# RWKV-7 block inverse: levels 2 to 16 kept as 32x32 diagonal blocks and multiplied in four array positions

## The chip, the cores and the metric

One NeuronCore of a Trainium2 chip runs the kernel. The metric is the device time of one execution in microseconds (us), as the median of a few runs. Engines are named as in the profile: PE is TensorE's matmul stream, PEld its weight loads, DVE is VectorE, ACT is ScalarE, POOL is GpSimd and SP is SyncE, which issues the DMAs of the weight stream.

## What is computed

Two layers of a hybrid decoder trunk on 256 tokens, in float32. Each layer has one input projection that feeds three head groups (HGRN2, latent attention called MLA, RWKV-7), an output projection, and a SwiGLU FFN. Only the RWKV-7 recurrence matters for the change:

```python
def step(state, inp):
    r_t, w_t, k_t, v_t, kk_t, a_t = inp
    sa = jnp.einsum('bhvk,bhk->bhv', state, -kk_t)
    state = (state * w_t[:, :, None, :]
             + sa[..., :, None] * (kk_t * a_t)[..., None, :]
             + v_t[..., :, None] * k_t[..., None, :])
    return state, jnp.einsum('bhvk,bhk->bhv', state, r_t)
```

with 8 heads of 64 channels. The kernel cuts the 256 steps into 4 chunks of 64. Inside a chunk the dependence of `sa` on earlier `sa` is a system with a 64x64 unit lower triangular matrix, I + A, where A holds decayed products of `kk` with `kk*a`. The kernel needs (I + A)^-1 for 8 heads x 4 chunks = 32 such matrices in each layer.

## The kernel before

**Where the inverse lives.** A tile is 64 partitions (one of two heads) x 64 columns; 16 tiles lie side by side (`JC` = 16), and the two heads of a pair share the partitions 0 to 63 (`EVEN`) and 64 to 127 (`ODD`). All buffers named here are views of one SBUF tensor, so the trace calls them all `arena`: `mab` (A below the diagonal), `inv` (the inverse so far), `inv_t` (its transpose), `g_t` (an intermediate).

**How it is inverted.** First the 2x2 diagonal blocks are set up (L1452 to L1454). Then five levels, `RW_LEVELS = [2, 4, 8, 16, 32]`, each double the block size. A level k is two steps on PE: `level_g(k)` multiplies `mab` with `inv_t` into the PSUM banks 0 and 1, ACT copies this out with a factor of -1 (`gt_out(k)`, L800), `level_x(k)` multiplies `inv` with it into banks 2 and 3, and DVE writes the new blocks by a copy under a mask (`level(k)`, L1440) into `inv_t` and turns them into `inv` by 32x32 transposes (L1432). Each step goes in two halves of 8 tiles. For levels 2 to 16 (k = 0 to 3) the products are full 64x64 ones by `both_heads` (L1897), in two positions of the PE array: rows and columns 0 to 63 for the even head, 64 to 127 for the odd. Level 32 (k = 4) multiplies single 32x32 quarters by `quarters` (L1906), also in two positions. At levels 2 to 16 no nonzero value leaves the 32x32 diagonal blocks of a tile.

**What stands around it.** PE's order is written out by hand (L2009 to L2044): the level steps stand between the steps of latent attention (`k_turn`, `attend` L1852 and L1858, `p_turn` L1870, `mix` L1878 and L1879) and the RWKV products (`product` L1897, `stack` L1920). After `level_x(4)` follow the chunk loop (L2051) and then the output projection, whose matmuls stand at L1631 to L1633. DVE's order is at L1451 to L1491 (`score_add` L1335, `score_max` L1341, `probs` L1353 and L1358 between the levels), ACT's at L863 to L888 (`softmax` L762, `probs_out` L769, `mix_out` L775, `stacked` L786, and the sums `sa` at L885). Each engine runs its list in order and waits on semaphores; nothing overtakes. These three lines of ACT's list matter below:

```python
                mix_out(0)
                gt_out(3)
                probs_out(3)
```

`mix_out(0)` waits for `rw_ab_done`, which DVE gives after `probs(3)` (L1474). PE's `p_turn(1)` waits for DVE's `probs(1)`.

**Elsewhere** the kernel streams weights: SP loads `raw`, ACT rounds them to `w_hi` (L532), DVE takes the rest as `w_lo` (L1000), and PE multiplies three times. The ring of `w_hi` and `w_lo` has four halves and `raw` has four slots, so this work runs ahead by that much.

Of the kernel before, what the change touches and what calls it, by code (L numbers as in the profile page):

```python
# [29 lines left out]
U32 = mybir.dt.uint32  # L30
# [23 lines left out]
RC = 64  # L54
NC = SEQ // RC
JC = 4 * NC
# [61 lines left out]
def build(nc, stream, x_in, positions, params, consts, lora, gains, rows, out):  # L118
    with ExitStack() as ctx:
# [119 lines left out]
        g_t = at(RING_END + 9856, JC, RC)  # L239
        inv = at(RING_END + 10880, JC, RC)  # L240
# [16 lines left out]
        LOWER = [slice(32, 64), slice(96, 128)]  # L257

# [263 lines left out]
        def _(act):  # L522
# [75 lines left out]
            for l in range(DEPTH):  # L598
# [190 lines left out]
                def gt_out(k):  # L789
                    last = k == len(RW_LEVELS) - 1  # L790
                    for hf in range(2):
                        h8 = slice(8 * hf, 8 * hf + 8)
                        act.wait_ge(S("rw_gt_mm"), 10 * l + 2 * k + hf + 1)
                        if last:
                            g3 = bank(hf).rearrange("p (n t) -> p n t", n=8)
                            nc.scalar.activation(g_t[UPPER[0], h8, 32:64], g3[UPPER[0], :, 32:64], ACT.Copy, scale=-1.0)
                            nc.scalar.activation(g_t[UPPER[1], h8, 32:64], g3[UPPER[1], :, 32:64], ACT.Copy,
                                                 scale=-1.0).then_inc(S("rw_gt_ready"), 1)
# [82 lines left out]
                gt_out(4)  # L881
                stacked(2, k_st, 4)
# [86 lines left out]
        def _(dve):  # L969
# [87 lines left out]
            def tables():  # L1057
# [7 lines left out]
                v(cp(lev_lo, flipped))  # L1065
                v(cp(small[:, 202:204], small[:, 200:202].bitcast(I32)))
# [35 lines left out]
            for l in range(DEPTH):  # L1102
# [305 lines left out]
                v(tt(rw_a, rw_a, rw_kk, MUL))  # L1408
# [25 lines left out]
                def level(k):  # L1434
                    last = k == len(RW_LEVELS) - 1
                    for hf in range(2):
                        h8 = slice(8 * hf, 8 * hf + 8)
                        dve.wait_ge(S("rw_dinv_mm"), 10 * l + 2 * k + hf + 1)
                        if not last:
                            vs(nc.vector.copy_predicated(inv_t[:, h8, :], over(lev_up[:, k, :], 8, RC).bitcast(U32),  # L1440
                                                         bank(2 + hf).rearrange("p (n t) -> p n t", n=8)),
                               "rw_xt", 12 * l + 2 * k + hf + 3)
                            vs(turn_blocks(inv[:, h8, :], inv_t[:, h8, :]), "rw_x", 10 * l + 2 * k + hf + 3)
                        else:
                            d3 = bank(2 + hf).rearrange("p (n t) -> p n t", n=8)
                            for up in UPPER:
                                u(cp(inv_t[up, h8, 32:64], d3[up, :, 32:64]))
# [164 lines left out]
        def _(pe):  # L1612
# [81 lines left out]
            for l in range(DEPTH):  # L1694
# [205 lines left out]

                def quarters(b0, ns, left, right):

                    last = None
                    for m, n in enumerate(ns):
                        for h in range(2):
                            last = mm(bank(b0)[UPPER[h], m * RC + 32:(m + 1) * RC], left(h, n), right(h, n),  # L1906
                                      start=True, stop=True)
                    return last
# [4 lines left out]

                def tile_of(z):
                    return lambda hp, n: z[hp, n, :]
# [10 lines left out]
                def level_g(k):  # L1926
# [3 lines left out]
                    for hf in range(2):  # L1930
                        ns = range(8 * hf, 8 * hf + 8)
                        pe.wait_ge(S("rw_xt"), 12 * l + 2 * k + hf + 1)
                        if last:
                            quarters(hf, ns, lambda h, n: mab[LOWER[h], n, 0:32],
                                     lambda h, n: inv_t[LOWER[h], n, 32:64]).then_inc(S("rw_gt_mm"), 1)
                        else:
                            both_heads(hf, ns, tile_of(mab), tile_of(inv_t), RC).then_inc(S("rw_gt_mm"), 1)

                def level_x(k):
                    last = k == len(RW_LEVELS) - 1  # L1940
                    for hf in range(2):
# [5 lines left out]
                        if not last:  # L1947
                            both_heads(2 + hf, ns, tile_of(inv), tile_of(g_t), RC).then_inc(S("rw_dinv_mm"), 1)
                        else:
                            quarters(2 + hf, ns, lambda h, n: inv[UPPER[h], n, 0:32],  # L1950
                                     lambda h, n: g_t[UPPER[h], n, 32:64]).then_inc(S("rw_dinv_mm"), 1)
# [119 lines left out]
                for c in range(NC):  # L2071
# [5 lines left out]
                    if c == 0:  # L2077
                        pe.wait_ge(S("rw_xt"), 12 * ev)
# [173 lines left out]
```

## Time and profile before

| what | us |
|---|---|
| runs | 2317.67, 2314.88, 2312.14 |
| median | 2314.88 |
| profiled execution: its own time | 2312.1 |
| its span, first to last instruction | 2309.8 |
| outside the span | 2.3 |

The span is 2.3 us shorter than the execution's own time. The profile has a page (busy time of the engines, the chain of work that ended last, groups of instructions) and views on the trace: groups by line, a timeline in order of time, sums over stretches. A busy PE counts the way of the last result through the array as well (a 64x64 matmul's record lasts 219 ns although the next starts long before), so the cost of a group of matmuls is read from its start to the start of the next group, and waits are read from the starts too. A float32 matmul leaves two records for each matmul in the code; `x64` in a row of L1897 is 32 matmuls.

### The profile page before, as it was taken

To read this page: it belongs to the slowest core of one execution; us is meant where nothing else is said; L and a number is where in the kernel's file an instruction comes from. 1 tells how busy PE (TensorE), PEld (TensorE's weight loads), DVE (VectorE), ACT (ScalarE), POOL (GpSimd) and SP (SyncE) were. 2 spreads that over 40 slices of the span, in tenths; PEclk is the share of its full clock that TensorE was granted. 3 is DMA by queue.
4 is the path that set the end of the run, shared out by engine and by line. 5 is a ranking of instruction groups with operands and counts; after the bars stand their busy time and mean duration, and the time that the engine had idled before them with its cause. 6 is when DMAs were issued, how large, how long until landed. Compare 5 with 4: busy or idle time off the path is not lost.

```text
span 2309.8 us, 32601 instructions
## 1 busy us (share of the span) xinstructions
PE 2285.3 (99%) x13153; PEld 1890.2 (82%) x13153; DVE 1377.5 (60%) x1504; ACT 1112.5 (48%) x1378; POOL 35.7 (2%) x50
## 2 busy tenths in 40 slices
PE   8999999999999999999999999999999999999999
PEld 7888688888888888888888886888888888888887
DVE  5787677655555445555657857775555554455554
ACT  6554755544444344444445547465444443444443
POOL 0000100000000000000000001000000000000000
PEclk9999999999999999999999999999999999999999
DMA  8555306656655555666655543156566565556553
GB/s 322 187 187 179 131 21 209 219 210 218 221 215 214 188 199 207 219 226 222 236 201 184 190 166 109 39 202 217 204 218 227 206 218 188 194 212 227 216 210 137
DMA packets 89041, 450.05 MB, mean 195 GB/s; under 512 B 9888, under 2 KB 30976, under 8 KB 42720
## 3 DMA queue, kind: packets, MB, share of 16 engines
q1 hardware_dynamic: 88240, 444.67, 54.3%
q0 software_dynamic: 688, 3.78, 0.5%
q8 instruction: 83, 1.36, 0.2%
q14 instruction: 30, 0.25, 0.0%
HBM read 424.82 MB, written 23.59 MB: 194 GB/s over the span
## 4 chain that ended last, share of the span: by engine, by line
PE 95%; DVE 3%; ACT 1%; DMA 0%; issue 0%; SPq 0%; DVEq 0%; ACTq 0%
PE psum L1631 29%; PE psum L1633 29%; PE psum L1632 29%; PE psum L1802 2%; PE psum L1897 2%; PE psum L2051 1%; PE psum L1726 1%; PE psum L1852 1%; DMA x<-x_in_dram 0%; PE psum L1858 0%; PE psum L1665 0%; DVE arena L1408 0%; PE psum L1906 0%; DVE arena L1410 0%; DVE arena L1414 0%
## 5 line engine op out<-in xcount | busy, mean ns | idle before, releaser
L1000 DVE TENSOR_TENSOR w_lo<-raw,w_hi 128x1024 fp32r<-128x1024 f32 (+2 forms) x752 | 901.1, 1205 | 756.1 <-ACT w_hi L532 745.9
L532 ACT ACTIVATE w_hi<-raw 128x1024 fp32r<-128x1024 f32 (+2 forms) x752 | 783.6, 1045 | 1045.0 <-PE psum L1633 1042.9
L1631 PE MATMUL psum<-w_hi,hT_hi 128*128 128x512 f32 (+2 forms) x2128 | 820.2, 385 | 5.0 <-DVE w_lo L1000 5.0
L1633 PE MATMUL psum<-w_hi,hT_lo 128*128 128x512 f32 (+2 forms) x2128 | 816.8, 384 | 0.0
L1632 PE MATMUL psum<-w_lo,hT_hi 128*128 128x512 f32 (+2 forms) x2128 | 816.8, 384 | 0.0
L1631 PEld LDWEIGHTS psum<-w_hi,hT_hi 128*128 128x128 f32 x2128 | 400.5, 188 | 84.0 <-DVE w_lo L1000 4.2
L1633 PEld LDWEIGHTS psum<-w_hi,hT_lo 128*128 128x128 f32 x2128 | 400.4, 188 | 78.1
L1632 PEld LDWEIGHTS psum<-w_lo,hT_hi 128*128 128x128 f32 x2128 | 400.5, 188 | 77.3
L1631 PE MATMUL psum<-w_hi,act_hi 128*128 128x512 f32 x872 | 339.2, 389 | 0.0
L1632 PE MATMUL psum<-w_lo,act_hi 128*128 128x512 f32 x872 | 339.2, 389 | 0.0
L1633 PE MATMUL psum<-w_hi,act_lo 128*128 128x512 f32 x872 | 339.2, 389 | 0.0
L1632 PEld LDWEIGHTS psum<-w_lo,act_hi 128*128 128x128 f32 x872 | 163.7, 188 | 34.0
L1631 PEld LDWEIGHTS psum<-w_hi,act_hi 128*128 128x128 f32 x872 | 163.7, 188 | 33.9
L1633 PEld LDWEIGHTS psum<-w_hi,act_lo 128*128 128x128 f32 x872 | 163.7, 188 | 33.9
L1802 PE MATMUL psum<-raw,arena 128*128 128x384 f32 (+1 forms) x192 | 71.9, 525 | 0.4
L1802 PEld LDWEIGHTS psum<-raw,arena 128*128 128x128 f32 x192 | 35.3, 190 | 30.9 <-issue 11.8
L1897 PEld LDWEIGHTS psum<-arena 64*64 64x64 f32 x1536 | 46.7, 135 | 10.4 <-DVE arena L1417 4.0
L1897 PE MATMUL psum<-arena 64*64 64x64 f32 x1536 | 49.9, 219 | 4.7 <-DVE arena L1417 2.3
L1564 DVE TENSOR_TENSOR act_lo<-gain,act_hi 128x1024 f32 (+1 forms) x22 | 27.0, 1226 | 21.0 <-ACT act_hi L949 21.0
L1547 DVE SCALAR_TENSOR_TENSOR act_row<-psum,small,silu 128x512 f32<-128x512 f32 x44 | 30.9, 744 | 0.0
L1054 DVE TENSOR_TENSOR x<-x,psum 128x1024 f32<-128x1024 f32 x23 | 27.9, 1214 | 4.9 <-PE psum L1633 4.9
L1554 DVE STREAM_TRANSPOSE gain<-act_row 128x1024 f32<-128x1024 f32 x22 | 27.4, 1245 | 3.3 <-DVE act_row L1547 1.7
(316 smaller groups left out, 1107.8 us busy)
## 6 DMA issues: line engine op xcount, KB each, us to landing
raw<-stream_dram SPq DMA_DIRECT2D x360, 1024.0 KB, 4.8
bounce<-gain SPq DMA_DIRECT2D x164, 128.0 KB, 2.7
gain<-bounce SPq DMA_DIRECT2D x41, 512.0 KB, 3.3
raw<-stream_dram SPq DMA_DIRECT2D x16, 512.0 KB, 5.0
raw<-stream_dram SPq DMA_DIRECT2D x8, 768.0 KB, 6.3
raw<-stream_dram SPq DMA_DIRECT2D x8, 640.0 KB, 3.9
x<-x_in_dram SPq DMA_DIRECT2D x4, 512.0 KB, 9.3
lor<-lora_dram POOLq DMA_DIRECT2D x2, 832.0 KB, 10.8
```

What stands on the lines that cost most here:

```text
L532: nc.scalar.activation(w_hi[:, q % HALF_RING, 0:2 * w], raw[:, j % 4, hf * 2 * w:(hf + 1) * 2 * w], ACT.Copy).then_inc(hi_done, 1)
L1000: tt(w_lo[:, q % HALF_RING, 0:2 * w], raw[:, j % 4, hf * 2 * w:(hf + 1) * 2 * w], w_hi[:, q % HALF_RING, 0:2 * w].bitcast(F32), SUB).then_ ...
L1054: vs(tt(xs, xs, psum[:, b0:b0 + 2, :], ADD), "x_added", n_added)
L1547: last = stt(act_row.rearrange("p a b -> p (a b)").rearrange("p (n t r) -> p t n r", n=16, t=TT)[:, t], psum[:, 2 + t, :].rearrange("p (n ...
L1554: nc.vector.transpose(blocks.rearrange("p (q k n) -> p k q n", q=4, k=4), act_row.rearrange("p a b -> p (a b)").rearrange("p (k q n) -> p ...
L1564: tt(lo, moved.rearrange("p (b n e) -> p n b e", n=8, e=32), hi.bitcast(F32), SUB).then_inc(S("act_lo_ready"), 1)
L1631: mm(o, a_hi, w_hi[:, r, cols], start=(k == 0), stop=False)
L1632: mm(o, a_hi, w_lo[:, r, cols], start=False, stop=False)
L1633: last = mm(o, a_lo, w_hi[:, r, cols], start=False, stop=(k == n_k - 1))
L1726: last = mm(bank(b0)[half, n * RC:(n + 1) * RC], left[:, h, tok], right[:, h, tok], start=True, stop=True)
L1802: last = mm(psum[:, UP_BANK[c] + t, 0:w], src[:, k, t * P:(t + 1) * P], raw[:, c % 4, k * w:(k + 1) * w], start=(k == 0), stop=(k == nk - 1))
L1897: last = mm(bank(b0, 2)[hp, m * w:(m + 1) * w], left(hp, n), right(hp, n), start=True, stop=True)
```

## The change

The level steps 2 to 16 keep and multiply only the two 32x32 diagonal blocks of each tile. `inv`, its transpose (now a buffer of its own, `inv_d`) and `g_t` are 32 columns wide instead of 64: the 128 partitions are four quarters, and each holds one diagonal block.

- PE: `half_blocks` makes four 32x32 matmuls for each tile of 8, one in each of four array positions (partitions 32q to 32q+31 in, the same out), where `both_heads` made two of 64x64. Level 32 stays in `quarters`, with its operands at new places.
- ACT: `gt_out` copies 128x256 instead of 128x512. A new `inverse_out`, between `gt_out(4)` and `stacked(2)`, puts the diagonal blocks into `inv_t`: one copy of 128x512 with a factor for each partition, and two of 32x512. `inv_t` is complete after it, so `rw_xt` counts 13 instead of 12 in a layer.
- DVE: the set-up of the 2x2 blocks is an addition of 128x512 that makes the identity, two masked copies of 128x512 and one transpose of 128x512; it was a product and a scalar_tensor_tensor of 128x1024 and a transpose of 128x1024. In the levels the masked copy and the transpose are 128x256 instead of 128x512. The factor -1 moves out of `gt_out` and of `rhs` into `rw_a`: `tensor_tensor` becomes `scalar_tensor_tensor` there, and `rhs` is a plain copy. Once at the start of the program the two halves of the level masks are added (128x128).

```diff
-        g_t = at(RING_END + 9856, JC, RC)
-        inv = at(RING_END + 10880, JC, RC)
+        HB = RC // 2
+        g_t = at(RING_END + 9856, JC, HB)
+        inv = at(RING_END + 10880, JC, HB)
+        inv_d = at(RING_END + 10880 + JC * HB, JC, HB)
...
+        QUARTER = [slice(32 * q, 32 * q + 32) for q in range(4)]
+        IN_HALF = [slice(32 * (q % 2), 32 * (q % 2) + 32) for q in range(4)]
...
                         if last:
-                            g3 = bank(hf).rearrange("p (n t) -> p n t", n=8)
-                            nc.scalar.activation(g_t[UPPER[0], h8, 32:64], g3[UPPER[0], :, 32:64], ACT.Copy, scale=-1.0)
...
                         else:
-                            nc.scalar.activation(g_t[:, h8, :].rearrange("p a b -> p (a b)"), bank(hf),
-                                                 ACT.Copy, scale=-1.0).then_inc(S("rw_gt_ready"), 1)
+                            nc.scalar.activation(g_t[:, h8, :], g3, ACT.Copy).then_inc(S("rw_gt_ready"), 1)
+
+                def inverse_out():
+
+                    act.wait_ge(S("rw_xt"), 13 * l + 10)
+                    nc.scalar.activation(inv_t[:, :, 0:32], inv_d, ACT.Copy, scale=C("strict_up")[:, 32:33])
+                    for low in LOWER:
+                        last = nc.scalar.activation(inv_t[low, :, 32:64], inv_d[low], ACT.Copy)
+                    last.then_inc(S("rw_xt"), 1)
...
                 gt_out(4)
+                inverse_out()
                 stacked(2, k_st, 4)
...
+                v(tt(lev_up[:, :, 0:32], lev_up[:, :, 0:32], lev_up[:, :, 32:64], ADD))
...
-                v(tt(rw_a, rw_a, rw_kk, MUL))
+                v(stt(rw_a, rw_a, -1.0, rw_kk, MUL, MUL))
...
                         if not last:
-                            vs(nc.vector.copy_predicated(inv_t[:, h8, :], over(lev_up[:, k, :], 8, RC).bitcast(U32),
-                                                         bank(2 + hf).rearrange("p (n t) -> p n t", n=8)),
-                               "rw_xt", 12 * l + 2 * k + hf + 3)
-                            vs(turn_blocks(inv[:, h8, :], inv_t[:, h8, :]), "rw_x", 10 * l + 2 * k + hf + 3)
+                            vs(nc.vector.copy_predicated(inv_d[:, h8, :], over(lev_up[:, k, 0:32], 8, HB).bitcast(U32), d3),
+                               "rw_xt", 13 * l + 2 * k + hf + 3)
+                            vs(turn_blocks(inv[:, h8, :], inv_d[:, h8, :]), "rw_x", 10 * l + 2 * k + hf + 3)
...
+                v(tt(inv, over(idst[:, 0:32], JC, HB), over(idst[:, 32:64], JC, HB), ADD))
                 dve.wait_ge(S("rw_m_mm"), 4 * l + 1)
-                v(tt(inv, bank(2, 2).rearrange("p (n t) -> p n t", n=JC), over(C("pair_lo"), JC, RC), MUL))
-                vs(stt(inv, inv, -1.0, over(idst, JC, RC), MUL, ADD), "rw_x", 10 * l + 1)
-                vs(turn_blocks(inv_t, inv), "rw_xt", 12 * l + 1)
+                a3 = bank(2, 2).rearrange("p (n t) -> p n t", n=JC)
+                v(nc.vector.copy_predicated(inv, over(C("pair_lo")[:, 0:32], JC, HB).bitcast(U32), a3[:, :, 0:32]))
+                vs(nc.vector.copy_predicated(inv, over(C("pair_lo")[:, 32:64], JC, HB).bitcast(U32), a3[:, :, 32:64]),
+                   "rw_x", 10 * l + 1)
+                vs(turn_blocks(inv_d, inv), "rw_xt", 13 * l + 1)
...
-                dve.wait_ge(S("rw_xt"), 12 * ev)
+                dve.wait_ge(S("rw_xt"), 13 * ev)
...
-                    vs(ts(rhs.rearrange("p a b -> p (a b)"), bank(0)[:, 0:256], -1.0, None, MUL), "rw_rhs_ready", NC * l + c + 1)
+                    vs(cp(rhs.rearrange("p a b -> p (a b)"), bank(0)[:, 0:256]), "rw_rhs_ready", NC * l + c + 1)
...
+                def half_blocks(b, ns, left, right):
+
+                    last = None
+                    for m, n in enumerate(ns):
+                        for q, rows in enumerate(QUARTER):
+                            last = mm(bank(b)[rows, m * HB:(m + 1) * HB], left(q, n), right(q, n), start=True, stop=True)
+                    return last
...
-                            both_heads(hf, ns, tile_of(mab), tile_of(inv_t), RC).then_inc(S("rw_gt_mm"), 1)
+                            half_blocks(hf, ns, lambda q, n: mab[QUARTER[q], n, IN_HALF[q]],
+                                        lambda q, n: inv_d[QUARTER[q], n, :]).then_inc(S("rw_gt_mm"), 1)
...
-                            both_heads(2 + hf, ns, tile_of(inv), tile_of(g_t), RC).then_inc(S("rw_dinv_mm"), 1)
+                            half_blocks(2 + hf, ns, lambda q, n: inv[QUARTER[q], n, :],
+                                        lambda q, n: g_t[QUARTER[q], n, :]).then_inc(S("rw_dinv_mm"), 1)
```

The order of the engines' lists stays. On PE, at level 2 of the first layer (`level_g(0)`, `k_turn(1)`, `level_x(0)`), there stood before (line 1897 is `both_heads`, 1822 is `k_turn`):

```order
L1897 MATMUL psum<-arena 64x64 [waits rw_xt,rw_m_ready,rw_stacked]
L1897 MATMUL psum<-arena 64x64 x15
L1897 MATMUL psum<-arena 64x64 [waits rw_xt]
L1897 MATMUL psum<-arena 64x64 x15
L1822 MATMUL psum<-con,arena 128x128 [waits mla_rT_ready,mla_k_normed]
L1822 MATMUL psum<-con,arena 128x128 x7
L1897 MATMUL psum<-arena 64x64 [waits rw_m_ready,rw_x,rw_gt_ready]
L1897 MATMUL psum<-arena 64x64 x15
```

and now stand (line 1920 is `half_blocks`, 1836 is `k_turn`):

```order
L1920 MATMUL psum<-arena 32x32 [waits rw_xt,rw_m_ready,rw_stacked]
L1920 MATMUL psum<-arena 32x32 x31
L1920 MATMUL psum<-arena 32x32 [waits rw_xt]
L1920 MATMUL psum<-arena 32x32 x31
L1836 MATMUL psum<-con,arena 128x128 [waits mla_rT_ready,mla_k_normed]
L1836 MATMUL psum<-con,arena 128x128 x7
L1920 MATMUL psum<-arena 32x32 [waits rw_m_ready,rw_x,rw_gt_ready]
L1920 MATMUL psum<-arena 32x32 x31
```

Twice as many matmuls stand in each half, 32 for 16, with the same waits at the same places.

On ACT, at level 32 of the first layer, from the rounding of two weight halves (line 532) through `gt_out(4)` (796 and 797) and `stacked(2)` (786) to the first `sa` (885), there stood before:

```order
L532 ACTIVATE w_hi<-raw 128x1024 [waits half_used,raw_in0] x2
L796 ACTIVATE arena<-psum 32x8x32 [waits rw_gt_mm]
L797 ACTIVATE arena<-psum 32x8x32
L796 ACTIVATE arena<-psum 32x8x32 [waits rw_gt_mm]
L797 ACTIVATE arena<-psum 32x8x32
L786 ACTIVATE arena<-psum 64x8x64 [waits rw_stack_mm]
L786 ACTIVATE arena<-psum 64x8x64 x3
L885 ACTIVATE arena<-psum 128x256 [waits rw_sa_mm]
```

and now stand (808 and 810 are `inverse_out`, 790 is `stacked(2)`, 896 the first `sa`):

```order
L536 ACTIVATE w_hi<-raw 128x1024 [waits half_used,raw_in0] x2
L800 ACTIVATE arena<-psum 32x256 [waits rw_gt_mm]
L801 ACTIVATE arena<-psum 32x256
L800 ACTIVATE arena<-psum 32x256 [waits rw_gt_mm]
L801 ACTIVATE arena<-psum 32x256
L808 ACTIVATE arena<-arena,con 128x16x32 [waits rw_xt]
L810 ACTIVATE arena<-arena 32x16x32 x2
L790 ACTIVATE arena<-psum 64x8x64 [waits rw_stack_mm]
L790 ACTIVATE arena<-psum 64x8x64 x3
L896 ACTIVATE arena<-psum 128x256 [waits rw_sa_mm]
```

Three copies stand ahead of `stacked(2)`; the wait of the first of them is for the end of level 16.

## Rows read from the trace of the kernel before

**Rows 1.** The page: busy time of PE, and the chain that ended last, by engine.

```profile
PE 2285.3 (99%) x13153; PEld 1890.2 (82%) x13153; DVE 1377.5 (60%) x1504; ACT 1112.5 (48%) x1378; POOL 35.7 (2%) x50
...
PE 95%; DVE 3%; ACT 1%; DMA 0%; issue 0%; SPq 0%; DVEq 0%; ACTq 0%
```

**Rows 2.** Sums over the stretch in either layer: length, busy, then PE clock, DMA.

```profile
281.34:349.22 67.88, 64.72 (x1539) 58.45 (x1539) 51.27 (x91) 36.38 (x75) 0.00 (x0) 1.00 0.10 34
1429.69:1497.57 67.88, 64.72 (x1539) 58.45 (x1539) 51.28 (x91) 36.38 (x75) 0.00 (x0) 1.00 0.09 32
```

**Rows 3.** Timeline of PE, first layer: start us, length us, engine, line.

```profile
289.72 2.08 PE L1897 MATMUL psum<-arena 64*64 64x64 f32 x64 [0.25 <-ACT arena L786]
291.74 1.09 PE L1822 MATMUL psum<-con,arena 128*128 128x128 f32 x8
...
297.13 1.58 PE L1852 MATMUL psum<-arena 128*128 128x128 f32 x8
...
305.88 1.53 PE L1870 MATMUL psum<-con,arena 128*128 128x128 f32 x12
...
308.71 3.02 PE L1897 MATMUL psum<-arena 64*64 64x64 f32 x96 [0.22 <-DVE arena L1440]
311.66 0.87 PE L1870 MATMUL psum<-con,arena 128*128 128x128 f32 x6
...
314.62 0.38 PE L1879 MATMUL psum<-arena 128*128 128x128 f32 x2
314.84 0.60 PE L1878 MATMUL psum<-arena 128*128 128x256 f32 x2
...
319.85 2.08 PE L1897 MATMUL psum<-arena 64*64 64x64 f32 x64 [0.72 <-ACT arena L800]
...
326.69 1.20 PE L1906 MATMUL psum<-arena 32*32 32x32 f32 x64
327.82 2.08 PE L1897 MATMUL psum<-arena 64*64 64x64 f32 x64
...
338.04 0.63 PE L2051 MATMUL psum<-gain,arena 64*64 64x64 f32 x16
338.51 0.63 PE L2051 MATMUL psum<-arena,con 64*64 64x64 f32 x16
```

**Rows 4.** Groups by line and form, 281 to 350 us: busy us, mean ns.

```profile
L1440 DVE COPY_PREDICATED arena<-con,psum 128x512 f32<-128x512 uint32 x8 | 5.9, 735 | 1.3 <-PE psum L1897 0.9
L1432 DVE STREAM_TRANSPOSE arena<-arena 128x512 f32<-128x512 f32 x8 | 5.7, 712 | 0.3
L800 ACT ACTIVATE arena<-psum 128x512 f32<-128x512 f32 x8 | 4.5, 593 | 2.8 <-PE psum L1897 2.8
L1484 DVE TENSOR_SCALAR arena<-psum 128x256 f32<-128x256 f32 x4 | 1.7, 425 | 3.2 <-PE psum L2051 2.9 <-DVEq L1449 0.2
L885 ACT ACTIVATE arena<-psum 128x256 f32<-128x256 f32 x4 | 1.5, 384 | 11.5 <-PE psum L2051 11.5
L1453 DVE SCALAR_TENSOR_TENSOR arena<-arena,con 128x1024 f32<-128x1024 f32 x1 | 1.2, 1226 | 0.0
```

**Rows 5.** Timeline of DVE, from score_add(1) to level 4's first masked copy.

```profile
297.33 0.96 DVE L1335 TENSOR_TENSOR arena<-psum,con 128x768 f32<-128x768 f32 x1 [0.37 <-PE psum L1858]
...
303.99 0.96 DVE L1335 TENSOR_TENSOR arena<-psum,con 128x768 f32<-128x768 f32 x1 [0.56 <-PE psum L1858]
...
306.40 0.74 DVE L1440 COPY_PREDICATED arena<-con,psum 128x512 f32<-128x512 uint32 x1
```

**Rows 6.** Timeline of ACT: stacked(1); mix_out(0) and gt_out(3); stacked(2).

```profile
287.06 2.40 ACT L786 ACTIVATE arena<-psum 64x512 f32<-64x512 f32 x4
...
318.29 1.02 ACT L775 ACTIVATE hT_hi<-psum 128x1024 fp32r<-128x1024 f32 x1 [2.79 <-DVE arena L1474]
319.21 1.08 ACT L800 ACTIVATE arena<-psum 128x512 f32<-128x512 f32 x2
...
330.96 2.40 ACT L786 ACTIVATE arena<-psum 64x512 f32<-64x512 f32 x4 [1.77 <-PE psum L1920]
```

More of the change, by code:

```diff
@@ L793, in gt_out @@
                         act.wait_ge(S("rw_gt_mm"), 10 * l + 2 * k + hf + 1)
+                        g3 = bank(hf)[:, 0:8 * HB].rearrange("p (n t) -> p n t", n=8)
                         if last:
-                            g3 = bank(hf).rearrange("p (n t) -> p n t", n=8)
-                            nc.scalar.activation(g_t[UPPER[0], h8, 32:64], g3[UPPER[0], :, 32:64], ACT.Copy, scale=-1.0)
-                            nc.scalar.activation(g_t[UPPER[1], h8, 32:64], g3[UPPER[1], :, 32:64], ACT.Copy,
-                                                 scale=-1.0).then_inc(S("rw_gt_ready"), 1)
-                        else:
-                            nc.scalar.activation(g_t[:, h8, :].rearrange("p a b -> p (a b)"), bank(hf),
-                                                 ACT.Copy, scale=-1.0).then_inc(S("rw_gt_ready"), 1)
+                            nc.scalar.activation(g_t[UPPER[0], h8, :], g3[UPPER[0]], ACT.Copy)
+                            nc.scalar.activation(g_t[UPPER[1], h8, :], g3[UPPER[1]], ACT.Copy).then_inc(S("rw_gt_ready"), 1)
+                        else:
+                            nc.scalar.activation(g_t[:, h8, :], g3, ACT.Copy).then_inc(S("rw_gt_ready"), 1)
[5 more added lines that the diff above has]
+                    last.then_inc(S("rw_xt"), 1)
                 up_out(0)
@@ L1905, in quarters @@
                         for h in range(2):
-                            last = mm(bank(b0)[UPPER[h], m * RC + 32:(m + 1) * RC], left(h, n), right(h, n),
+                            last = mm(bank(b0)[UPPER[h], m * HB:(m + 1) * HB], left(h, n), right(h, n),
                                       start=True, stop=True)
@@ L1931, in level_g @@
                         ns = range(8 * hf, 8 * hf + 8)
[L1932 removed]
+                        pe.wait_ge(S("rw_xt"), 13 * l + 2 * k + hf + 1)
                         if last:
                             quarters(hf, ns, lambda h, n: mab[LOWER[h], n, 0:32],
[L1935 removed]
+                                     lambda h, n: inv_d[LOWER[h], n, :]).then_inc(S("rw_gt_mm"), 1)
                         else:
[L1937 removed]
+                            half_blocks(hf, ns, lambda q, n: mab[QUARTER[q], n, IN_HALF[q]],
+                                        lambda q, n: inv_d[QUARTER[q], n, :]).then_inc(S("rw_gt_mm"), 1)
                 def level_x(k):
@@ L1947, in level_x @@
                         if not last:
-                            both_heads(2 + hf, ns, tile_of(inv), tile_of(g_t), RC).then_inc(S("rw_dinv_mm"), 1)
-                        else:
-                            quarters(2 + hf, ns, lambda h, n: inv[UPPER[h], n, 0:32],
-                                     lambda h, n: g_t[UPPER[h], n, 32:64]).then_inc(S("rw_dinv_mm"), 1)
+                            half_blocks(2 + hf, ns, lambda q, n: inv[QUARTER[q], n, :],
+                                        lambda q, n: g_t[QUARTER[q], n, :]).then_inc(S("rw_dinv_mm"), 1)
+                        else:
+                            quarters(2 + hf, ns, lambda h, n: inv[UPPER[h], n, :],
+                                     lambda h, n: g_t[UPPER[h], n, :]).then_inc(S("rw_dinv_mm"), 1)
                 up(0)
@@ L2077, in _ @@
                     if c == 0:
-                        pe.wait_ge(S("rw_xt"), 12 * ev)
+                        pe.wait_ge(S("rw_xt"), 13 * ev)
                     elif c < NC - 1:
```

6 lines of the change are left out of this document (2 added, 4 removed).

## The prediction

> **What bounds the kernel now.** I read the page first. PE is busy 99% of the span and makes 95% of the chain that ended last [rows 1]. So a microsecond that PE's list loses is won, and one that another engine loses is won only where PE waits for it. The work that the change touches stands in one stretch of 67.88 us in either layer, with the same counts and sums to 0.01 us; what I find for the first layer counts twice. The granted clock is 1.00 there, the upper of TensorE's two levels, and the DMA engines are nearly idle [rows 2]. Next I read PE's timeline in the stretch. It is almost a list without gaps: it waits 0.25 us for ACT's `stacked(1)`, 0.22 at level 8 for DVE and 0.72 at level 16 for ACT's `gt_out(3)` [rows 3], and at a few other places. PE is thus the bound, but DVE is busy 51 of 68 us [rows 2] and stands close behind.
>
> **A step of a level on PE, before.** `level_g(0)` starts at 289.72 and the next group at 291.74: 2.02 us for 32 matmuls, 64 records [rows 3]. There are eight such steps in a layer (levels 2 to 16, g and x), 16 in all. The records come in rounds, one in each of the two array positions. In the chunk loop, where the shape doesn't change from group to group, 16 records take 0.47 us (338.04 to 338.51), so a round of 64 columns is 58.5 ns; 32 rounds are 1.87, and 0.15 is left for the change of shape at the start [rows 3].
>
> **The same step after.** 64 matmuls, 128 records of 32x32. The only rows with this shape are `quarters`: 64 records in two positions take 1.13 us (326.69 to 327.82), less 0.13 for the change of shape 1.00 us, or 31.3 ns for a round of two [rows 3]. A round of 64 columns costs 58.5 and one of 32 columns 31.3, so a column costs 0.85 ns and a round 4 ns besides: the time goes with the columns that stream through, and hardly with the number of instructions. The question is what a round of four positions costs, and no row shows one. Three values:
> - All four run side by side as two do now: 32 rounds of 31.3 ns are 1.00 us, the step 1.13.
> - All four run side by side but each position adds its own fixed part. With one position, 128 columns take 110 ns a record (two records, 314.62 to 314.84 [rows 3]), which is 109 by the 0.85 and thus 1 over; two positions are 4 over, so four may be some 10: 37 ns a round, the step 1.31.
> - Only two run at a time: 64 rounds, 2.00 us, the step 2.13.
> Rounds of two start within one column time of the other and keep their own pace; I see nothing in the rows that ties one position to the other but this small fixed part. I take 1.21, between the first two, as it lies nearest to the row with the same shape. PE's list then loses 8 x (2.02 - 1.21) = 6.5 us in each layer.
>
> Here a rule of the skill speaks against the change. The rows show two 32x32 positions with different rows of the array that write the same PSUM bank at 31.3 ns a round [rows 3], too short for one after the other, at 27 ns of columns each. The Trainium skill, TensorEngine Tiling (Array Packing), section Gotcha 1: PSUM Pressure, says that different row tiles cannot access the same PSUM bank simultaneously. By that rule the four would queue; by the rows they don't, and I hold with the rows.
>
> **What of the 6.5 us arrives.** I went through the stretch with the waits that each list has, and find five places.
> - Start. DVE's set-up before `mab` was two operations and a transpose of 128x1024 at about 1.23 us each, 3.7 in all; now four of 128x512 at 0.71 to 0.74, 2.9 [rows 4]. It gives `mab` 0.8 us sooner, but PE also waits for ACT's `stacked(1)`, which ends at 287.06 + 2.40 = 289.46 [rows 6], and starts at 289.72 now [rows 3]: 0.2 won.
> - After `level_x(0)`, `attend(1)` waits for `k_out(1)` on ACT, a copy of 128x1024 as `mix_out` is, 1.02 us [rows 6], that starts when `k_turn(1)` ends. `level_x(0)` covers it now with 2.0 us and will with 1.2: 0.1 to 0.2 lost.
> - `p_turn(1)`. From `score_add(1)` at 297.33 to the first masked copy at 306.40, DVE works through two `score_max`, two `probs` and three `score_add` with one wait of 0.56 [rows 5]: 8.5 us of work that the change does not shorten, and it starts when `attend(1)` is done. PE needs from `attend(2)` at 297.13 to `p_turn(1)`, half through the 1.53 us from 305.88 [rows 3], 9.5 us now and 9.5 - 1.6 = 7.9 after. So PE waits some 0.9 us: two steps give 0.7 instead of 1.6. The DVE chain takes the place of PE there.
> - Level 16. `gt_out(3)` stands behind `mix_out(0)` on ACT, and that waits for DVE's L1474, which follows `probs(3)`, `softmax(3)`, `probs_out(2)` and PE's `p_turn(2)`. From `p_turn(2)` at 311.66 to `level_x(3)` at 319.85 are 8.19 us [rows 3] of which PE's own work is not the bound; they stay, less 0.2 for the shorter `gt_out(3)`. Of the 0.8 us of `level_g(3)` 0.2 arrives: 0.6 lost.
> - Level 8. The wait of 0.22 before its second half shrinks with the shorter masked copy and gives 0.1 to 0.3, and the next three waits, on `gt_out(2)` and `probs(2)`, take 0.2 to 0.3 back: nothing.
> Sum: 6.5 + 0.2 - 0.15 - 0.9 - 0.6 = 5.05; I take 4.9 for small waits that I can't place.
>
> **The other edits.** The masked copies and transposes of the levels are half as long in elements. 128x512 takes 0.735 and 0.712; another operation of DVE takes 0.425 at 128x256 [rows 4], so I put them at 0.43 to 0.49. That saves DVE 0.5 us a level, of which only the wait at level 8 was on PE's path. `gt_out` falls from 0.59 to the 0.38 of `sa`, which has the same shape [rows 4]; PE waited for it only where counted. `inverse_out` is three copies on ACT, 0.59 for 128x512 and not less than 0.38 nor more than 0.6 for each of the two on 32 partitions: 1.4 to 1.8 us, ahead of `stacked(2)`. ACT sat idle for 1.77 us before `stacked(2)` until PE's `stack` was done [rows 6], so it is hidden to within 0.1. It opens with `rw_xt` at the end of level 16, long past. Behind it are queued `stacked(2)` and the first `sa`; DVE waits for it before `rhs`, which comes 2 us after. Without this cover each microsecond of it would stand before the chunk loop. The factor in `rw_a` costs nothing: scalar_tensor_tensor over 128x1024 takes 1.226 us [rows 4], as a tensor_tensor of that size would by DVE's 0.71 to 0.74 for half the elements. The plain copy for `rhs` is at worst the same. The mask addition runs once, under 0.4 us, while PE works on the first weights. After the stretch nothing changes but the start: the weight halves are rounded ahead of it by up to four, and PE's list stays the bound, so the gain is kept to the end.
>
> **The sum** against the profiled execution: 2312.1 - 2 x 4.9 = 2302.3 us. That execution lies 2.8 us below the median of the runs shown; the median I expect is 2314.9 - 9.8 = 2305.1.
>
> **Rivals.**
> 1. Four positions run side by side, but instructions come too slowly to feed them. The rows show 128 loads and matmuls in 1.00 us [rows 3] and no higher rate; at four positions it would be twice that. A pace of 45 to 50 ns a round of four gives a step of 1.57 to 1.73, and 3.6 to 2.6 us a layer: 2308 to 2310. For it: the rate is unseen. Against: time went with columns, so the present rate is no limit.
> The Trainium skill, TensorE: Matmul & The Clock Gate, section Wait — 56ns, not 53.3ns?, gives a floor of about 25 ns from matmul to matmul. Taken for a float32 matmul with its two records, that would be 1.6 us a step, an estimate that lies within this rival; taken for each record, the rows at 15.7 ns already deny it.
> 2. Only two positions run at a time. The step is 2.13 us, 0.9 us more on PE in a layer, against 0.2 won at the start, 0.2 at level 8 and 0.2 at level 16, with small waits gone: within 0.5 us, 2314 to 2316. For it: two is all the rows show. Against: nothing in them hints at a limit of two.
> 3. The positions queue up behind each other in the bank that they share, as the Gotcha says. 128 records of 27 + 2 ns are 3.8 us a step, 1.9 more; 16 steps cost 30, less some 3 for what other waits absorb: 2342. It turns from gain to loss at a step of 2.14 us, 15.7 ns a record, which is today's pace of two at a time; anything slower loses. For it: four writers to a bank are new. Against: two writers show no queue.
> 4. The change does what it says on PE but DVE and ACT give nothing: the `probs(1)` chain decides more than I think. It runs from `attend(1)` alone, so it can take at most the 1.6 us of two steps, another 0.7 us a layer: 2306.5, inside the forecast's range.
>
> **Chances.** The forecast with four side by side (steps of 1.13 to 1.31 us and rival 4) 0.68: 2302 to 2308 with the runs' own spread. Rival 1 0.12, rival 2 0.13, rival 3 and other losses 0.07. A measurement tells 0.2%, 4.6 us, from no change. Rival 1 lies to two thirds above that bound. Faster 0.77, same 0.15, slower 0.08. The range from 2301 to 2314 leaves out rival 3, most of rival 2 and a tail of luck.
>
> **What would show it.** The rows of `half_blocks` should last from start to start 1.13 to 1.31 us for 128 records; 2.1 or 3.9 would be rivals 2 and 3, 1.6 rival 1. PE should wait about 0.9 us in `p_turn(1)` for DVE and 1.3 to 1.5 before `level_x(3)` for ACT. The stretch should be 4.9 us shorter in both layers and `stacked(2)` start as soon as `stack` is done. A lower granted clock in the stretch, a wait of PE before the chunk loop, or a gap at the first weights of the output projection would each make the prediction wrong.

## The result, and the profile of the changed kernel

The changed kernel is slower: median 2322.74 us (2319.49 to 2327.64, 7 runs) against 2312.14 us (2310.73 to 2317.67, 7 runs) for the kernel before, a ratio of 1.0043 with a 95% interval of 1.0028 to 1.0057. The prediction was 2305.1 us, faster: 9.8 us under the 2314.9 of the three runs known then. The profiled execution took 2319.49 us with a span of 2317.2, so it is the shortest of the seven.

First the page of the changed kernel: busy time and counts, the instruction queue of the DMA part, and the chain by engine. They answer to [rows 1], where PE had 13153 matmul records.

```profile
PE 2281.5 (98%) x14177; PEld 1883.9 (81%) x14177; DVE 1366.5 (59%) x1507; ACT 1112.4 (48%) x1384; POOL 35.7 (2%) x50
...
q8 instruction: 91, 1.49, 0.3%
...
PE 95%; DVE 3%; issue 1%; ACT 1%; DMA 0%; SPq 0%; DVEq 0%; ACTq 0%
```

PE has less busy time than before (2281.5 against 2285.3 us) in a longer span, and the chain now has 1% of "issue", time in which PE waited for nothing that the profile names. The page of the kernel before has this queue row:

```profile
q8 instruction: 83, 1.36, 0.2%
```

Eight packets more and 0.13 MB more, for 1024 matmul records and 1024 weight loads more: one packet of 16 KB is 256 instructions. The next view, the waits of PE in the changed kernel (line waited at, releaser, us in total, times, longest), says where "issue" stands: L1920 is the matmul of `half_blocks`.

```profile
PE psum L1920 <- issue: 12.4, 10, 2.5
PE psum L1645 <- DVE w_lo L1011: 5.6, 4, 1.9
```

The stretches from the product to the first weights of the output projection, as [rows 2]: length, then busy us and count of PE, PEld, DVE, ACT and POOL, PE's clock, DMA share, GB/s.

```profile
282.96:354.42 71.46, 62.83 (x2050) 55.42 (x2051) 45.98 (x92) 36.83 (x78) 0.00 (x0) 0.95 0.09 33
1434.90:1504.99 70.09, 61.51 (x2050) 54.42 (x2050) 45.97 (x92) 36.75 (x78) 0.00 (x0) 0.98 0.09 32
```

They are 3.6 and 2.2 us longer than the 67.88 of before, where 4.9 us less was forecast, and the clock is no longer 1.00. PE's timeline in the first layer, answering to [rows 3], shows both things at once:

```profile
291.14 1.31 PE L1920 MATMUL psum<-arena 32*32 32x32 f32 x128
292.38 1.09 PE L1836 MATMUL psum<-con,arena 128*128 128x128 f32 x8
293.40 0.34 PE L1920 MATMUL psum<-arena 32*32 32x32 f32 x17
294.48 1.23 PE L1920 MATMUL psum<-arena 32*32 32x32 f32 x111 [0.74 <-issue]
...
302.05 0.33 PE L1920 MATMUL psum<-arena 32*32 32x32 f32 x16 [0.51 <-issue]
302.31 1.58 PE L1866 MATMUL psum<-arena 128*128 128x128 f32 x8
303.82 0.93 PE L1872 MATMUL psum<-arena 64*128 64x128 f32 x8
304.67 1.65 PE L1920 MATMUL psum<-arena 32*32 32x32 f32 x128
306.26 1.78 PE L1884 MATMUL psum<-con,arena 128*128 128x128 f32 x12
307.97 1.06 PE L1920 MATMUL psum<-arena 32*32 32x32 f32 x82
310.10 1.41 PE L1920 MATMUL psum<-arena 32*32 32x32 f32 x127 [1.08 <-issue]
314.05 0.64 PE L1920 MATMUL psum<-arena 32*32 32x32 f32 x47 [2.53 <-issue]
...
317.06 1.22 PE L1892 MATMUL psum<-arena 128*128 128x256 f32 x2 [0.90 <-ACT arena L773]
...
326.23 0.91 PE L1920 MATMUL psum<-arena 32*32 32x32 f32 x76 [1.59 <-issue]
```

- Where nothing interrupts it, the step is as forecast: from 291.14 to 292.38, 1.24 us for 128 matmul records in four positions (1.21 forecast, 2.02 before).
- Other steps are cut in the middle, after 17 or 112 or 82 records. Nothing in the program stands there. Between two such gaps PE always got a multiple of 256 instructions: from 302.05 to 310.10 the rows hold 16 + 8 + 8 + 128 + 12 + 82 = 254 matmuls, with their weight loads 508, and with the 4 semaphore instructions between them 512; from 310.10 to 314.05 they hold 127 matmuls, with loads and 2 semaphore instructions 256. The gaps stand at the borders of the packets of 256.
- The gaps in this layer add up to 6.45 us (0.74, 0.51, 1.08, 2.53, 1.59), in the second to 5.94.

The DMA view of the changed kernel between 290 and 330 us, in which little but instructions is moved (GB/s in 40 slices of 1 us; 16 is one packet of 16 KB):

```profile
GB/s 0 0 16 0 0 16 0 0 0 16 0 0 0 16 0 0 0 16 0 0 0 16 0 0 0 16 0 0 0 0 0 0 0 16 0 0 0 16 8 0
```

and the same view of the kernel before:

```profile
GB/s 0 16 0 0 0 16 0 0 0 0 0 0 0 0 0 16 0 0 0 0 16 0 0 0 0 0 0 0 16 0 0 0 0 0 0 16 0 8 0 16
```

Before, the fetches (the packets' own records in the trace give their starts) come 3.5 to 10 us apart from 291 to 330 us. In the changed kernel they follow one another every 3.5 to 4.1 us without a break up to the half-clock stretch (starts at 292.15, 295.61, 299.66, 303.43, 307.24, 311.16, 315.10 us), while a packet itself takes 0.9 to 1.4 us. I call this the supply: PE gets at most one block of 256 instructions in about 3.8 us. In none of the traces of this study do two fetches start less than 3.3 us apart. PE can use up 256 four-position instructions in 1.24 us.

The packets and the gaps belong together one by one. Each of the ten gaps ends 1.2 to 1.5 us after a packet has arrived: the packets that start at 307.24 and 311.16 are in at 308.66 and 312.51, and PE goes on at 310.10 and 314.05. The next packet starts 1.05 to 1.4 us after PE has gone on.

The Trainium skill, Runtime: NRT & Kernel Launch, section Instruction fetch mechanics, says that an engine's instructions come in 16 KiB blocks of 256 and that the cost of crossing from block to block is mostly hidden. The trace agrees with the block; with the second part it doesn't here, where ten crossings cost 12.4 us.

The last view is PE alone in four windows of the changed kernel (length, busy and count, granted clock, DMA share, GB/s):

```profile
291.00:301.00 10.00, 9.22 (x372) 1.00 0.02 5
301.00:311.00 10.00, 8.24 (x410) 1.00 0.02 3
311.00:321.00 10.00, 6.57 (x119) 0.67 0.02 3
321.00:331.00 10.00, 8.41 (x322) 0.98 0.02 4
```

The clock falls from the upper to the lower of its two levels after the gaps of 1.08 and 2.53 us, and stays there from about 314.5 to 321.3 us. The `mix` rows from 317.06 on then take nearly twice their time (1.22 and 1.06 us for two matmuls, where at the upper level it is 0.70 and 0.60).

So for the first layer: steps 8 x (2.02 - 1.24) = 6.2 us won; gaps 6.5 lost; in the half-clock stretch `p_turn` takes 1.54 instead of 0.87 and `mix(0)` 4.88 us (317.06 to 321.94) instead of 2.81 (309.87 to 312.68 in the timeline of experiment two), 2.7 lost. That is +3.0 of the +3.6 measured.

### The profile page after: what moved, and what is told of

The parts are those of the page before. It is cut to its first block, busy times and chain, and to the rows that moved or that the text cites. A ratio compares the mean times of both kernels' runs of the same rounds, so it can differ in the third digit from the quotient of the medians.

```text
span 2317.2 us, 34658 instructions
## 1 busy us (share of the span) xinstructions
PE 2281.5 (98%) x14177; PEld 1883.9 (81%) x14177; DVE 1366.5 (59%) x1507; ACT 1112.4 (48%) x1384; POOL 35.7 (2%) x50
## 4 chain that ended last, share of the span: by engine, by line
PE 95%; DVE 3%; issue 1%; ACT 1%; DMA 0%; SPq 0%; DVEq 0%; ACTq 0%
PE psum L1645 29%; PE psum L1646 29%; PE psum L1647 29%; PE psum L1816 2%; PE psum L2072 1%; PE psum L1920 1%; PE psum L1911 1%; PE psum L1740 1%; PE psum L1892 0%; PE psum L1866 0%; PE psum L1884 0%; PE psum L1679 0%; PE psum L1872 0%; DMA x<-x_in_dram 0%; DVE arena L1420 0%
## 5 line engine op out<-in xcount | busy, mean ns | idle before, releaser
L1920 PE MATMUL psum<-arena 32*32 32x32 f32 x2048 | 23.6, 194 | 12.6 <-issue 12.4
L1920 PEld LDWEIGHTS psum<-arena 32*32 32x32 f32 x2048 | 20.8, 105 | 17.3 <-issue 15.7
```

The source lines that it names most:

```text
L1920: last = mm(bank(b)[rows, m * HB:(m + 1) * HB], left(q, n), right(q, n), start=True, stop=True)
```

## The experiments

My theory after the result was the supply. The rivals were that the other edits cost the time, that four positions disturb each other in the array or the bank, and that the clock falls because of the small tiles and not because of the gaps.

**One. Only PE's part of the change.** Matrices stay 64 columns wide; ACT and DVE are those of before. `FOUR` lists all eight steps here.

```diff
+        FOUR = [('g', 0), ('g', 1), ('g', 2), ('g', 3), ('x', 0), ('x', 1), ('x', 2), ('x', 3)]
...
+                def half_blocks(b, ns, left, right):
+                    for m, n in enumerate(ns):
+                        for q, rows in enumerate(QUARTER):
+                            last = mm(bank(b)[rows, m * RC + IN_HALF[q].start:m * RC + IN_HALF[q].stop],
+                                      left[QUARTER[q], n, IN_HALF[q]], right[QUARTER[q], n, IN_HALF[q]], start=True, stop=True)
...
+                        elif ("g", k) in FOUR:
+                            half_blocks(hf, ns, mab, inv_t).then_inc(S("rw_gt_mm"), 1)
```

> Before, with one thing changed: levels 2 to 16 are multiplied as 32x32 blocks in four array positions (256 records of weights and matmuls in a level's half-step pair instead of 128), while the matrices stay 64 columns wide and ScalarE and VectorE do what they did before; no inverse_out. Theory 1 (supply): TensorE gets its instructions in blocks of 256, one block at most every 3.4 to 4.1 us, and the 1024 more instructions of a layer cannot be had in the time; the stalls come with the number of instructions alone. It expects what the changed kernel shows: gaps of TensorE that nothing else ends ('issue'), together 8 us or more in the new line, some 512 instructions apart, and a time 2 to 10 us over before (2314 to 2322 us). Rival 2 (the other edits): the loss comes from the extra ScalarE copies, the added VectorE addition or the sign that moved, and four positions by themselves are worth 0.8 us in each of the eight steps: it expects about 3 us less per layer than before, 2305 to 2308 us, and no issue gaps.

Measured: 2323.2 us (2320.09 to 2327.82, 4 runs) against 2313.44 (15 runs), ratio 1.0043, 1.0028 to 1.0059. PE's waits of this kernel (L1909 is `half_blocks` here) and its windows over the stretches:

```profile
PE psum L1909 <- issue: 9.8, 10, 2.5
...
PE psum L2067 <- issue: 1.9, 1, 1.9
```

```profile
282.88:357.97 75.09, 65.01 (x2051) 57.45 (x2051) 51.24 (x91) 36.28 (x75) 0.00 (x0) 0.91 0.09 32
1438.42:1513.28 74.86, 66.62 (x2051) 58.37 (x2051) 51.24 (x91) 36.45 (x75) 0.00 (x0) 0.89 0.08 30
```

The whole loss, at the same ratio, without one edit of ACT or DVE; the time is 1.2 us over the range that the supply theory gave. Rival 2 of the expectation, the other edits, is out. One gap, of 1.9 us, stands outside the levels, in the chunk loop (L2067), whose matmuls are those of before. The stretches are longer than in the changed kernel, and the clock in them is lower still (0.91 and 0.89); this profiled execution, 2327.82 us, is also the longest of the four.

**Two. Half the instructions, the same columns.** In the changed kernel only every second tile's weights are loaded, and the matmul runs over two tiles' columns. What it computes is not the inverse.

```diff
-                    for m, n in enumerate(ns):
+                    for m, n in list(enumerate(ns))[::2]:
                         for q, rows in enumerate(QUARTER):
-                            last = mm(bank(b)[rows, m * HB:(m + 1) * HB], left(q, n), right(q, n), start=True, stop=True)
+                            last = mm(bank(b)[rows, m * HB:(m + 2) * HB], left(q, n), right(q, slice(n, n + 2)),
+                                      start=True, stop=True)
```

> The changed kernel, but in levels 2 to 16 only every second tile is loaded as weights, and its matmul runs over the 32 columns of two tiles (64 columns): the same positions, PSUM banks and columns in sum, the same ScalarE and VectorE work, half the TensorE instructions. What is multiplied is not what the reference wants (the second tile of each pair is multiplied by the first one's weights); it measures time only. Theory 1 (supply of instruction blocks): the gaps go nearly to nothing, the clock stays at full speed, the steps still take about 1.2 us and the time is 4 to 5 us per layer under before: 2301 to 2306 us. Rival 3 (the array: four positions disturb one another or their writes into one bank do, so that the gaps are of the array): the gaps stay, time within 3 us of the changed kernel's 2323. Rival 4 (the clock falls because little of the array is lit by 32x32 tiles, and the gaps are not the cause): the gaps may go, but the granted clock still falls to half near 315 us and 1468 us; 2308 to 2316 us.

Measured: 2301.1 us (2300.2 to 2304.4, 5 runs), ratio 0.9956, 0.9942 to 0.9969. Its instruction queue on the page, its waits and its stretches:

```profile
q8 instruction: 83, 1.36, 0.2%
```

```profile
PE psum L1920 <- ACT arena L803: 3.0, 2, 1.5
PE psum L1884 <- DVEq L1372: 2.3, 2, 1.2
...
PE psum L1920 <- issue: 0.4, 1, 0.4
```

```profile
282.07:344.45 62.38, 57.45 (x1539) 50.39 (x1539) 46.03 (x92) 36.62 (x78) 0.00 (x0) 1.00 0.11 37
1423.39:1486.57 63.18, 57.69 (x1538) 50.48 (x1538) 46.01 (x92) 36.63 (x78) 0.00 (x0) 1.00 0.09 34
```

With the number of blocks back at 83 the gaps are gone but for one of 0.4 us, a step of 64 records takes 1.02 us (290.25 to 291.27), and the stretches are 5.5 and 4.7 us under before. All the rest of the change is in this kernel: four positions, one bank, the narrower copies, `inverse_out`. So neither positions nor bank are at fault. The clock is 1.00 with 32x32 weights in the same positions (each now with 64 columns), so small tiles alone don't lower it.

**Three. The same instructions, a slower step.** The changed kernel with positions 0 and 2 of all tiles first, then 1 and 3, so that two at most overlap.

```diff
-                    for m, n in enumerate(ns):
-                        for q, rows in enumerate(QUARTER):
+                    for two in ((0, 2), (1, 3)):
+                        for m, n in enumerate(ns):
+                            for q in two:
```

> The changed kernel with the products of a half-step in another order: first the positions 0 and 2 of all eight tiles, then the positions 1 and 3, so that two positions at most work side by side; the same instructions in number and kind. Theory 1 (supply): the half-steps take about as long as before (2.1 us a step), which leaves time for the blocks to come: the gaps fall from 12 us to under half of it, and the time is that of the slower steps, 2314 to 2322 us, about the changed kernel's although the array needs 7 us more per layer. Rival 5 (a fixed price for each gap or for each of the 91 blocks, whatever the pace): the gaps stay at about 12 us and the 16 slower steps come on top of them, 2335 us or more. Rival 3 (four positions collide): the gaps go and the time falls to 2310 to 2312 us.

Measured: 2324.35 us (2324.01 to 2325.61, 4 runs), ratio 1.0055, 1.0039 to 1.0070. Its waits, and a step in its timeline:

```profile
PE psum L1921 <- issue: 7.5, 8, 2.1
```

```profile
320.18 1.93 PE L1921 MATMUL psum<-arena 32*32 32x32 f32 x128
322.05 0.88 PE L1884 MATMUL psum<-con,arena 128*128 128x128 f32 x6
```

A step now takes 1.87 us instead of 1.24, 0.63 more, which over 16 steps is 10 us of PE work, and yet the ratio is 1.0055 where it was 1.0043, some 3 us. So most of it went into what had been gap or other waits: the gaps fell from 12.4 to 7.5 us. I had expected a step of 2.1 us, gaps under half, and a time up to 2322; all three missed by a little, the gaps and the time in the theory's direction but not by its numbers. The clock fell here too (0.95 and 0.91 over the stretches). The rivals' numbers, 2335 or more and 2310 to 2312, are far off.

**Four. Half the extra instructions, by another way to multiply.** The first product of each level takes 64x64 weights again, with A's off-diagonal corner in a buffer of its own and zero in A, and 32 compact columns; the second product stays in four positions. What it computes is the inverse again.

```diff
+        corner = at(RING_END + 9856 + JC * HB, JC, HB)
...
+                act.wait_ge(S("rw_m_ready"), 4 * l + 1)
+                nc.scalar.activation(corner, bank(2, 2).rearrange("p (n t) -> p n t", n=JC)[:, :, 0:32], ACT.Copy)
                 gt_out(0)
...
-                            half_blocks(hf, ns, lambda q, n: mab[QUARTER[q], n, IN_HALF[q]],
-                                        lambda q, n: inv_d[QUARTER[q], n, :]).then_inc(S("rw_gt_mm"), 1)
+                            both_heads(hf, ns, lambda hp, n: mab[hp, n, :],
+                                       lambda hp, n: inv_d[hp, n, :], HB).then_inc(S("rw_gt_mm"), 1)
...
-    out["strict_lo"] = a > b
+    out["strict_lo"] = (a > b) & (a // 32 == b // 32)
```

> The changed kernel, but the first product of each level 2 to 16 (A times the inverse) uses 64x64 weights again, with the off-diagonal corner of A kept in a small buffer of its own (one ScalarE copy more per layer) and zero in A; its moving side stays the 32 compact columns. The result is the reference's. This product needs 128 instructions per step as before, the second one 256 in four positions: 512 instructions more than before per layer instead of 1024. Theory 1 (supply): half the extra blocks, gaps of 2 to 4 us per layer instead of 5 to 6, 1.5 to 3.8 us per layer under before: 2305 to 2309 us. The step with 64x64 weights and 32 columns takes 1.0 to 1.3 us by the same theory, since its columns are half those of before. Rival 3 (four positions collide): half the loss of the changed kernel remains, 2314 to 2318 us. Rival 6 (a matmul of 32 columns behind 64-wide weights costs as much as 64 columns, 2.0 us per step): 2309 to 2313 us.

Measured: 2309.55 us (2306.49 to 2311.75, 11 runs), ratio 0.9986, 0.9977 to 0.9995: a little faster than before. Its timeline (the step with 64x64 weights and 32 columns, then the second product), its waits for "issue", and its stretches:

```profile
300.36 2.06 PE L1914 MATMUL psum<-arena 64*64 64x32 f32 x64
302.34 1.58 PE L1869 MATMUL psum<-arena 128*128 128x128 f32 x8
```

```profile
PE psum L1923 <- issue: 1.4, 1, 1.4
```

```profile
283.09:347.88 64.79, 61.92 (x1795) 55.66 (x1795) 45.98 (x92) 37.42 (x79) 0.00 (x0) 1.00 0.10 36
1426.87:1493.65 66.78, 62.33 (x1794) 55.79 (x1795) 45.99 (x92) 37.42 (x79) 0.00 (x0) 1.00 0.09 33
```

The stretches are 3.1 and 1.1 us under before; one long gap is left, in the second layer, where 2 to 4 us per layer were expected; the first product's step, slower than expected, leaves more time for the blocks. The time is 0.6 us over the range of the supply theory and inside that of rival 6, and on the step rival 6 is right: 32 columns behind 64-wide weights take 1.98 us from start to start (300.36 to 302.34), as 64 columns do. I had expected 1.0 to 1.3.

**Five. Half the extra instructions, spread.** Before, with four positions in only four of the eight steps: where PE's neighbouring rows are long, so that blocks can catch up.

```diff
+        FOUR = [('g', 1), ('g', 2), ('x', 0), ('x', 3)]
...
+                        elif ("g", k) in FOUR:
+                            half_blocks(hf, ns, mab, inv_t).then_inc(S("rw_gt_mm"), 1)
...
+                        if ("x", k) in FOUR:
+                            half_blocks(2 + hf, ns, inv, g_t).then_inc(S("rw_dinv_mm"), 1)
```

> Before, with the four-position product in only four of the eight steps of a layer: the first product of levels 4 and 8 and the second product of levels 2 and 16, those that stand where TensorE's rows around them are long (scores, mix), while the other steps keep 64x64 blocks; matrices 64 columns wide, ScalarE and VectorE as before, the reference's result. 512 instructions more per layer, as in the kernel with two positions in the first product, but spread. Theory 1 (supply, one block of 256 instructions per 3.8 us with at most one in hand): a stall remains in the dense places, 1.2 to 1.5 us per layer are kept, 2.6 us of the before: 2309 to 2312 us, issue gaps under 3 us in both layers together. A theory in which the number of blocks alone counts (each of the four more blocks costs what the eight cost in the run where only TensorE's steps were changed, 1.2 us) expects 4 x 1.2 us on top of the before's 2313.4: 2318 us. A theory without supply expects 4 x 0.8 us per layer off, 2307 us, and no gaps.

Measured: 2308.67 us (2306.9 to 2312.52, 11 runs), ratio 0.9982, 0.9973 to 0.9991. The stretches:

```profile
281.26:347.31 66.05, 62.36 (x1794) 55.75 (x1795) 51.26 (x91) 36.38 (x75) 0.00 (x0) 1.00 0.10 36
1426.27:1492.47 66.20, 62.47 (x1795) 55.85 (x1795) 51.26 (x91) 36.38 (x75) 0.00 (x0) 1.00 0.09 33
```

The page has 87 blocks, four more than before, and no wait for "issue" is among PE's. The time is 0.3 us under the supply theory's range; the theory that each extra block has a price (2318) is refuted. The third theory of the expectation, without any supply limit (2307 us and no gaps), is not: 2308.67 lies between the two, and there are no gaps. This run alone doesn't tell them apart; experiments one and two do. Together with them it says that what counts is how many instructions PE wants within the time of one block, not how many there are in all. This version and the one before it both beat the two kernels; their intervals overlap, so which of them is better stays open, and with it whether the choice of the four steps matters.

## Why the prediction was wrong

- **The four-position step** was right: 1.24 us measured, 1.21 forecast, and no sign of rivals 2 and 3. Experiment two shows four positions side by side without the supply's gaps. Queueing in the shared bank, the reading that the prediction took from the Trainium skill, TensorEngine Tiling (Array Packing), section Gotcha 1: PSUM Pressure, would have made 3.8 us of it; the rows deny it. One reading on the way was wrong and did no harm: the two matmuls of a round start 6 ns apart in the trace of before (326.774 and 326.780), some seven times the 0.85 ns of a column and not within one.
- **What arrives of it** was right in its places. From the product to `level_g(0)` there are 8.18 us (282.96 to 291.14) instead of 8.38 (281.34 to 289.72), the forecast 0.2 at the start. In experiment two the wait in `p_turn(1)` is 1.2 us (0.9 forecast) and that before `level_x(3)` 1.5 us (1.3 to 1.5 forecast), the DVE and ACT rows of its waits above. Its stretches are 5.5 and 4.7 us shorter, forecast 4.9, with a step that is 0.2 us shorter still.
- **The failed step** is the one that dismissed rival 1: "time went with columns, so the present rate is no limit". The rows did show PE at a higher rate than the 64 instructions a microsecond of the old step, but only in runs of 128 instructions, half a block (the `quarters`, 1.13 us). I asked how fast two instructions can follow each other, and the limit is how fast blocks of 256 can. Rival 1 had the right resource and the wrong shape: an even pace of 1.57 to 1.73 us a step, and so a gain of 2.6 to 3.6 us a layer. What the runs showed is an undisturbed step of 1.24 us and stalls of up to 2.5 us at block borders, 6.5 and 5.9 us a layer, which takes all of the gain back. (Rival 1's 2308 to 2310 us also lay wholly under 2310.3, the bound of 4.6 us below 2314.9, and not to two thirds.)
- **It could have been read before.** In [rows 3] a step held 128 instructions in 2.02 us and now holds 256 in 1.24. The instruction queue's packets in the trace of before start at 325.80, 329.25, 332.95, 337.11, 341.19 and 345.14 us through level 32 and the chunk loop, 3.5 to 4.2 apart, almost as tight as in the changed kernel (3.3 at the least). PE runs there without a gap, with 336 matmuls and 333 weight loads in 10 us (334 to 344), a block in 3.8 us: that is the pace at which the blocks come in the changed kernel. The loop was close to the limit already, as its gap of 1.9 us in experiment one bears out; I never looked at that queue, since the DMA share in [rows 2] is small.
- **The clock** was named as something that would make the prediction wrong, without a chance of its own. In the stretches of the changed kernel and of experiments one and three it fell nine times, each time in a gap or within 2.1 us of the end of one, the smallest that stood alone being one of 1.65 us (experiment three, 312.13 us). It fell in no stretch where the gaps were gone or nearly so (two, four and five; the longest left there is 1.4 us, in four). That it follows from the gaps is the plain reading of this, but not every pause does it: in the kernel before PE waits 1.79 us for DVE ahead of the product of the second layer (1429.69 us), and the clock stays at 1.00. What else it takes is open; no run made such gaps by other means.
- **The other edits.** `inverse_out` took 1.99 us on ACT (0.72 + 1.27; forecast 1.4 to 1.8), from 334.41 to 336.42, and `stacked(2)` started at 336.44, right behind it. PE's `stack`, from 335.04 on, was done at about 336.13, so the cost is some 0.3 us of ACT (forecast 0.1 at most), and PE waits for `stacked(2)` nowhere. The masked copies take 0.443 and the transposes 0.445 us (forecast 0.43 to 0.49).
- **Open.** The two stretches explain 5.8 us of the difference; the profiled execution is 7.4 over that of before, and the medians are 10.6 apart. 1.6 us arise before 283 us, where the program differs by one mask addition: the clock between 225 and 235 us is 0.83 there and 1.00 in the kernel before, and it is 0.83 also in the profiles of experiments one and four and 1.00 in those of two, three and five. Experiments one and five run the same program up to there, and one shows 0.83 and the other 1.00: it comes and goes with the execution. The rest would be longer stretches in the other runs (their clocks go down to 0.993), as experiment one's profile shows with +7.2 and +7.0 us; what decides how much a run loses was not settled.

## What to carry to other kernels

When an edit makes matmuls smaller, count instructions in blocks as well as columns: here a block of 256 came at most every 3.3 to 4.1 us, so a stretch in which PE would use blocks faster stalls, whatever the array can do, and idle PE may then cost the clock too. The starts of the instruction queue's packets in the trace before tell where there is room. Put the smaller matmuls beside long ones, as in experiment five, or keep the count by giving a matmul more columns, where what is computed allows it (in experiment two it didn't).

## What the runs showed of the hardware

- PE's instructions come in packets of 16 KB for 256 instructions. A packet takes 0.9 to 1.8 us, but no packet started less than 3.3 us after the start of the last, even while PE stood still. All 32 gaps of PE that the stretches of the seven traces put down to "issue" end 1.2 to 1.6 us after a packet has arrived, and the next packet starts 1.0 to 1.9 us after that: the fetches follow one another as in a chain, and the packet is only about a third of the time. What happens in the two delays no run shows.
- Four 32x32 positions write one bank in 9.7 ns a record (128 in 1.24 us), two at a time in 14.6 ns (128 in 1.87 us, experiment three).
- In these rows a round's price goes with the wider of weights and columns. 64x64 weights take 1.98 us a step (32 rounds of two) with 32 columns and 2.02 with 64; 32x32 weights take 1.02 for 16 rounds of four with 64 columns (experiment two), so all three cost 62 to 64 ns a round; 32x32 weights with 32 columns take 1.13 for 32 rounds of two, 35 ns a round. The prediction's "a column costs 0.85 ns" compared two shapes in which both widths changed together, and can't be split so.
